# Rows of two expert matrices regrouped: eight neighbouring rows to a partition, and token copies in the same order

## What is computed

```python
t = modulate(rms_norm(x, norm2_g), sh2, sc2)        # (384, 1024)
# router: best of 4 groups, then the best 2 of its 4 experts, gives gate (384, 16), two entries a token
a = jnp.einsum("nd,edf->nef", t, moe_w1)            # (16, 1024, 512) weights, fp32
b = jnp.einsum("nd,edf->nef", t, moe_w3)            # (16, 1024, 512)
y = jnp.einsum("nef,efd->nd", silu(a) * b * gate[..., None], moe_w2)   # (16, 512, 1024)
x = x + g2 * y
```

## Time and profile before

| what | value |
|---|---|
| median of 3 runs | 1374.74 us (1372.54 to 1381.22) |
| profiled execution, its own time | 1372.78 us |
| span of its instructions | 1371.0 us |
| mean granted TensorE clock | 0.958 of full |
| TensorE matmul busy | 1256.0 us, 92% of the span |
| ScalarE busy | 310.4 us, 23% |
| read from memory | 318.64 MB |

### The profile page before, as it was taken

One profiled execution on the slowest core, in us unless ns is written; L12 is line 12 of the kernel. 1 busy time (PEld: TensorE's weight loads), 2 busy tenths in 40 slices (PEclk: granted clock), 3 DMA queues, 4 the chain that ended last, 5 costly groups with the idle time before them and its releaser, 6 DMA issues.

```text
span 1371.0 us, 21250 instructions
## 1 busy us (share of the span) xinstructions
PE 1256.0 (92%) x8943; PEld 616.6 (45%) x8943; DVE 577.2 (42%) x1478; ACT 310.4 (23%) x743; POOL 91.3 (7%) x104
## 2 busy tenths in 40 slices
PE   4999996899978999999989999969899699999996
PEld 1565544575553333333346554537556333333332
DVE  1266977464353212121262687945625412121215
ACT  0237412223131010101022661223322210101010
POOL 0020011110010000000021000021000100000001
PEclk9899998899988999999999999979999899999998
DMA  9550144868765999999675012275595589999994
GB/s 339 187 151 0 62 149 115 269 229 307 295 241 185 339 399 396 400 397 399 271 291 161 0 62 85 83 199 200 185 347 174 199 289 392 397 397 399 395 397 162
DMA packets 172690, 340.86 MB, mean 249 GB/s; under 512 B 34463, under 2 KB 36903, under 8 KB 172583
## 3 DMA queue, kind: packets, MB, share of 16 engines
q1 hardware_dynamic: 164807, 312.82, 63.5%
q0 software_dynamic: 7776, 26.55, 5.3%
HBM read 318.64 MB, written 20.71 MB: 248 GB/s over the span
## 4 chain that ended last, share of the span: by engine, by line
PE 71%; DVE 13%; DMA 9%; SPq 4%; issue 2%; ACT 1%; POOL 0%; POOLq 0%; DVEq 0%; ACTq 0%
PE bank L513 67%; PE bank L516 4%; DVE ring L1671 3%; DMA ring<-in_moe_w_dram 3%; DVE arena L1671 2%; DMA ring<-in_ada_w_dram 1%; DMA ring<-in_w_in_dram 1%; DVE arena L1679 1%; DVE small L1679 1%; DMA arena<-tok_dram,idx 1%; SPq L1255 1%; DMA raw_dram<-ring 1%; SPq L1202 1%; SPq L1213 1%; DVE x L1679 1%
## 5 line engine op out<-in xcount | busy, mean ns | idle before, releaser
L513 PE MATMUL bank<-ring,arena 128*32 128x512 f32 (+1 forms) x3088 | 469.6, 588 | 4.8 <-ACT arena L1363 2.9
L513 PE MATMUL bank<-arena 128*32 128x512 f32 (+4 forms) x2160 | 377.9, 530 | 28.8 <-DVE arena L1671 21.6
L1363 ACT ACTIVATE arena<-bank 128x512 f32<-128x512 f32 (+3 forms) x320 | 143.1, 479 | 612.6 <-PE bank L516 328.8
L513 PE MATMUL bank<-ring,hT 128*128 128x512 f32 x576 | 254.5, 597 | 2.4 <-DMA ring<-in_w_in_dram 2.4
L513 PEld LDWEIGHTS bank<-ring,arena 128*32 128x32 f32 (+1 forms) x3088 | 139.6, 114 | 223.0 <-issue 223.0
L513 PEld LDWEIGHTS bank<-arena 128*32 128x32 f32 (+3 forms) x2160 | 130.8, 127 | 162.8 <-issue 124.0
L513 PEld LDWEIGHTS bank<-ring,hT 128*128 128x128 f32 x576 | 108.2, 192 | 128.6 <-issue 125.8
L1671 DVE TENSOR_TENSOR hT<-hT,bank 128x512 f32<-128x512 f32 x24 | 16.5, 687 | 335.0 <-PE bank L513 335.0
L513 PE MATMUL bank<-hT,ring 128*128 128x384 f32 x384 | 132.3, 501 | 0.0
L513 PEld LDWEIGHTS bank<-hT,ring 128*128 128x128 f32 x384 | 73.7, 196 | 48.4 <-issue 4.2
L516 PE MATMUL bank<-const,arena 128*128 128x128 f32 x347 | 52.0, 288 | 33.4 <-DMA arena<-tok_dram,idx 19.6
(11 more groups left out here) (139 smaller groups left out, 905.7 us busy)
## 6 DMA issues: line engine op xcount, KB each, us to landing
ring<-in_moe_w_dram SPq DMA_DIRECT2D x62, 2048.0 KB, 16.7
arena<-in_moe_w_dram SPq DMA_DIRECT2D x34, 2048.0 KB, 18.6
ring<-in_ada_w_dram SPq DMA_DIRECT2D x24, 2048.0 KB, 8.9
ring<-in_w_in_dram SPq DMA_DIRECT2D x14, 2048.0 KB, 9.7
expert_dram<-arena SPq DMA_DIRECT2D x22, 512.0 KB, 15.9
ring<-in_w_out_dram SPq DMA_DIRECT2D x4, 2048.0 KB, 8.5
arena<-in_na_rpb_dram SPq DMA_DIRECT2D x32, 96.0 KB, 4.7
tok_dram<-arena POOLq DMA_DIRECT2D x6, 512.0 KB, 4.0
```

Of the source, the lines that this page charges most:

```text
L513: return nc.tensor.matmul(out, lhsT, rhs, start=start, stop=stop)
L1363: return nc.scalar.activation(out, in_, func, **kw)
```

## The change

The views of `moe_w1` and `moe_w3` put row `8 p + k` into partition p at step k, so that a partition's eight rows lie next to each other in memory: one piece of 16 KB a partition, 128 pieces a slab. `moe_w2` keeps its view. To match, column `128 k + p` of a token copy must hold feature `8 p + k`: `token_rows` on ScalarE reads the bank with a step of eight and writes eight runs of 64. TensorE's instructions, the gathers, the stores and all waits are as before. The same views serve the loads of the branch for overfull experts, which is not taken here.

```diff
-            EXPERT_W = [w.rearrange("l e (k p) n -> p (l e) k n", p=P) for w in (moe_w1, moe_w3, moe_w2)]
+            EXPERT_W = [w.rearrange("l e (p k) n -> p (l e) k n", p=P) for w in (moe_w1, moe_w3)]
+            EXPERT_W.append(moe_w2.rearrange("l e (k p) n -> p (l e) k n", p=P))
...
                 def token_rows(t):
                     for half in range(2):
                         b = filled("tok", l, t, half)
-                        f(tok_sb[:, t, half * 512:(half + 1) * 512], b[:]).then_inc(act_emptied, 1)
+                        dst = tok_sb[:, t, :].rearrange("p (k i) -> p k i", k=KC)[:, :, 64 * half:64 * half + 64]
+                        f(dst, b[:].rearrange("p (i k) -> p k i", k=KC)).then_inc(act_emptied, 1)
```

## The result

The changed kernel takes 1373.51 us (median of 20 runs, 1368.41 to 1377.04), the kernel before 1375.95 us (median of 20). The ratio is 0.9971, with a 95% interval from 0.9958 to 0.9984: about 4 us faster, between 2.2 and 5.8. The two medians alone differ by 2.4 us. The ratios are of fast runs only: one execution of the kernel before, 5363.84 us in the last group of runs, counts as slow and is left out.

A forecast was written before the change was run, and what follows sets the result against it. TensorE bounds the expert stages except for two load waits. 1372.78 - 1.95 + 0.4 = 1371.2 us from the profiled execution, 1373.2 us from the median of the runs shown; 1372 us was given, range 1365 to 1386 us.

The forecast's parts named there:

- The bound: Expert stages: TensorE is the bound at 22.48 us a batch, except two load waits at batch 9, 1.9 us together.
- The cost of a piece: Expert slab loads: 9.9 ns fixed plus 74.8 ns per 2 KB, so 608 ns for 16 KB, 431 GB/s against 387.
- The rival of pieces cut up: w1 and w3 loads: 16 KB fetched in portions as costly as before, no faster, 1373 us; chance 0.14.
- a slower order of addresses: w1 and w3 loads: engines walking separate 16 KB stretches get in each other's way; 1401 us at 340 GB/s; chance 0.12.
- What it is worth: Batch 9 of each layer: faster slab loads end TensorE's waits of 1.03 and 0.92 us, -1.95 us in all.
- The queues: SP's issues and gathers: 0 us; a gather may lose 4.7 us, landing after about 12 us, but stays hidden.
- The token copies: Twelve ScalarE copies reading PSUM with a step of eight: +0.1 us each, +0.4 us in all, high end +6.6 us.
- The rule on cachelines: Stepped PSUM reads in token copies: half-used 8-byte lines cost 1.7 us, high end 6.6; 1373 to 1377 us; chance 0.08.
- what covers the copies: Token copies: only tile 0's two lie on the path, since TensorE needs the banks back; tiles 1 and 2 are covered.
- The slow side: Expert loads in 1 KB pieces, expected before that experiment: 346 GB/s, 24 to 34 us more, ratio 1.017 to 1.025.

The follow-up runs named there:

- the ceiling run: Kernel before, but after layer 0's first eight slabs each expert load brings only the first half of its steps (1 MB, not 2): 1373.05 us, ratio 0.9971.
- The copies-only kernel: Kernel before with only the token copies changed to the stepped ones, loads as before: 1377.11 us beside 1376.95, ratio 0.9988.
- the 1 KB run: Kernel before with every expert slab loaded by two DMAs, w1 and w3 in 1 KB pieces, w2 in 2 KB pieces: 1407.16 us, ratio 1.0189.

## Why the prediction was right, point by point

**The forecast.** It said 1372 us within 1365 to 1386 and no change within 1%; 1373.51 us and a ratio of 0.9971 were measured. That the time came so near is partly luck: the median of three runs that it started from was 1.2 us below the median of 20, and the saving was put 0.9 us too low against the 2.4 us of the medians, and the two cancel.

**The bound.** Right. TensorE's 216.47 us is a floor that no load moves, seen in nine traces, and the batches stayed at 22.48 us.

**The cost of a piece.** Right, and beyond the sizes it was fitted to. The engines from 350 to 360 us in the changed kernel:

```profile
DMA packets 292, 4.26 MB, mean 426 GB/s; under 512 B 32, under 2 KB 32, under 8 KB 32
q1 hardware_dynamic: 292, 4.26, 99.9%
```

The 260 whole pieces in it took 0.999 x 160 us of engine time, 0.615 us each, where 608 ns were worked out. A fixed 9.9 ns and 74.8 ns for each 2 KB give 346, 424 and 431 GB/s at 1, 8 and 16 KB; measured were 348, 420 and 426 (in the same 10 us of three more traces with the changed loads 426, 424 and 434). The pieces stayed whole: exactly 57,344 packets fewer. The rival of pieces cut up falls, and so does that of a slower order of addresses.

**What it is worth.** The mechanism was right, the size a little low: the prediction gave -1.95 us to the waits and +0.4 us to the copies. The waits taken away are 2.09, 2.64 and 2.15 us in the three traces with 2 KB pieces (the excess over 2 x 216.47), 2.3 on average, where the one profile at hand showed 1.95. 2.3 us is a ratio of 0.9983, inside all three intervals of the changed kernel (0.9958 to 0.9984, 0.9956 to 0.9994, 0.9965 to 0.9991), at the edge of the first. Their centre, 0.9975, would be 3.4 us, while the medians of the same three pairs differ by 2.4, 2.6 and 2.9 us. The table shows no place for the missing 1 us, and the ceiling run none either, so whether it exists stays open. The copies-only kernel shows how far two measures of one pair can lie apart: its ratio is 0.9988, or 1.6 us faster, and its median 0.2 us slower.

**Where most of the saved DMA time went.** The loads of w1 and w3 take 0.5 us less each, some 32 us over both layers, and 2.3 us of it arrive. The rest becomes slack: the engines fall idle at the end of a layer's experts. Two windows of the changed kernel:

```profile
640.00:660.00 20.00, 20.00 (x188) 6.48 (x184) 3.33 (x4) 1.69 (x4) 0.00 (x0) 1.00 1.02 418
660.00:680.00 20.00, 20.00 (x192) 6.15 (x184) 4.00 (x5) 1.19 (x2) 0.00 (x0) 1.00 0.25 97
```

**The queues.** Right. The gathers, which take turns with the larger pieces, land later and TensorE waits for them no more than before (19.6 us for the first gathers of the two layers, in both kernels):

```profile
DMA to landing us min/median/max: 4.5/8.4/13.1
```

The median rose by 1.0 us and the longest from 8.5 to 13.1 us; about 12 were worked out if each packet stood behind a 16 KB piece. The Trainium skill says in "DMA: Bandwidth & Descriptors" (Queues, rings and completion order) that each engine goes round its queues a packet at a time; the rise agrees with that, the runs don't isolate it.

**The token copies.** The term of +0.4 us was wrong: two stepped copies take 1.08 us like two plain ones, so the term is 0. The rule on cachelines that the Trainium skill states in "SBUF — State Buffer", and that the prediction weighed, speaks of matmuls where it speaks of PSUM; on ScalarE reading PSUM 32 bytes apart no such effect shows, as the 1.08 us tell. The reading of what covers the copies failed too, without harm. I put tile 0's two copies on the path because TensorE needs the banks back. The copies in eight instructions took 0.9 us longer a tile and held TensorE up by 0.06 us behind each of tile 0 and tile 2. What is on the path in this stretch, and was in no term, is the clock: in layer 0 of most traces it falls to the lower level between 397 and 407 us. There the same 16 gate matmuls behind tile 2 take 1.95 us in three of the thirteen traces and 2.4 to 3.6 us in the other ten, with the plain copies as with the stepped ones. From tile 2's transposes to the first gather it takes 8.0 us where the clock stays up, 9.15 and 10.1 us in the two traces of the kernel before, and 9.4 us in that of the copies in eight.

**The slow side.** The price of a lower rate held in the 1 KB run: 24 to 34 us were expected and 26 measured. But the expected sum had only transfers in it, and 8.7 of the 28.5 us by which the two expert stages grew are the clock, five stretches of 1.7 to 1.8 us. So the size agrees in part by luck.

## What to carry to other kernels

Where two engines are both near full, look for who waits for whom, not for their shares: a transfer made 10% cheaper, in a stage where it runs at full load, was worth only the two waits that it ended, 2.3 us of 1374. Two piece sizes found in one trace give the cost of a third by a straight line, so the rate can be known before the change is built; what the rate is worth needs the lead of the buffers. And a run with half of the bytes gives the ceiling of every such idea at once. Before a longer row is put down to a wait, look at the granted clock of that window: the same 16 matmuls took 1.95 us or 3.58.

## What the runs showed that I had not expected

- A wait of TensorE can cost more than itself. In the 1 KB run, five gaps of 1.9 to 3.6 us were each followed by a stretch at the lower clock that cost another 1.7 to 1.8 us. Behind the gaps of 0.7 to 1.8 us in the three traces with 2 KB pieces, and behind one of 3.5 us in the 1 KB run, the clock stayed up.
- The clock goes with much of the scatter between runs. Over the 35, 23 and 28 counted runs of the kernel before in the three groups, a mean granted clock lower by 0.001 goes with a time longer by 0.8, 0.8 and 0.6 us (a straight line through each group). Which of the two brings the other, the runs don't tell.
- VectorE's last product of a layer starts 0.06 us, or 1.3 to 2.8 us, or 3.8 us after TensorE's end, and the profile names no instruction of the kernel that it waits for. The amount goes with the group of runs and not with the kernel: all four traces of one group show 1.3 and 2.3 to 2.5 us, all three of another 0.06, and in layer 1 all four of the third show 3.8 to 3.9 (in layer 0 three show 2.8 and one 1.4). The record has the same chip for the first two of these groups, so the chip alone doesn't set it. It makes up to 6.7 us of a span, more than the change. Its cause stays open.
- Eight short ScalarE copies in a row cost 0.98 us together, 0.12 us each, where one alone of 128 numbers takes 0.28 us: most of the fixed share overlaps.
